# Weights laid out on the host in 8 KB rows, the first modulation taken k-tile by k-tile, and the context rows asked for one weight piece later

## What is computed

```
mod_lat = (silu_c @ ada_w[i] + ada_b[i])          # 6 x 2048 numbers: shift, scale, gate, twice
mod_ctx = silu_cc @ ada_w[i] + ada_b[i]
h_lat = modulate(rms_norm(x, norm_mix_g[i]), sh1, sc1)      # h * (1 + scale) + shift
h_ctx = modulate(rms_norm(ctx, norm_mix_g[i]), csh1, csc1)
if mixer == 0:
    q_l, k_l, v_l = project_qkv(h_lat, attn_w_qkv[j], attn_q_norm_g[j], attn_k_norm_g[j])
    k_c, v_c = project_kv(h_ctx, attn_w_qkv[j][:, D_MODEL:], attn_k_norm_g[j])
    o_lat = latent_attention(q_l, k_l, v_l, k_c, v_c) @ attn_w_o[j]
else:
    o_lat = fourier_mix(h_lat, fourier_w_o[j])
x = x + g1 * o_lat
x = x + g2 * sq_relu_mlp(modulate(rms_norm(x, norm_mlp_g[i]), sh2, sc2), mlp_w1[i], mlp_w2[i])
```

## Time and profile before

| | us |
|---|---|
| median of three runs | 2005.79 |
| the profiled execution | 2005.52 |
| its span (first to last instruction) | 2003.6 |
| PE busy in the span | 1965.9 (98%) |
| DVE busy | 1391.5 (69%) |
| ACT busy | 969.3 (48%) |
| DMA, mean over the span | 271 GB/s |

### The profile page before, as it was taken

The page is one execution under the profiler, slowest core; times in us unless marked ns, Lnnn a source line. Parts: engine busy times, 40 slices in busy tenths (PEclk is TensorE's granted clock), DMA queues, the critical chain, the costliest instruction groups (busy, mean ns, idle before and its releaser), DMA issues.

```text
span 2003.6 us, 24992 instructions
## 1 busy us (share of the span) xinstructions
PE 1965.9 (98%) x10188; PEld 1609.5 (80%) x10188; DVE 1391.5 (69%) x1424; ACT 969.3 (48%) x1265; POOL 110.9 (6%) x196
## 2 busy tenths in 40 slices
PE   6999989999999999999999999999999999999998
PEld 4677756778888888888888888788888888888886
DVE  3666998889867787788888675766666455555556
ACT  6432565455544455544444464555554454444444
POOL 1111001000000000000000000000000000000000
PEclk9999999999999999999999999999999999999999
DMA  9998768779989899799999626577776566555653
GB/s 359 338 378 319 277 257 297 272 252 323 353 293 348 313 360 364 262 367 363 355 395 383 219 85 193 175 252 253 257 251 220 187 192 210 189 192 198 218 190 126
DMA packets 152261, 542.80 MB, mean 271 GB/s; under 512 B 9393, under 2 KB 10577, under 8 KB 114641
## 3 DMA queue, kind: packets, MB, share of 16 engines
q1 hardware_dynamic: 119312, 335.77, 47.9%
q0 software_dynamic: 31744, 201.34, 27.1%
q10 hardware_dynamic: 1090, 4.09, 0.5%
HBM read 535.91 MB, written 2.10 MB: 269 GB/s over the span
## 4 chain that ended last, share of the span: by engine, by line
PE 94%; DVE 3%; ACT 1%; DMA 1%; issue 1%; POOL 0%; ACTq 0%; DVEq 0%; POOLq 0%
PE ps L2098 13%; PE ps L2036 12%; PE ps L2032 12%; PE ps L2035 11%; PE ps L2096 11%; PE ps L2099 6%; PE ps L1848 6%; PE ps L2095 6%; PE ps L1849 5%; PE ps L1850 5%; PE ps L2257 1%; PE ps L1913 1%; PE ps L2204 1%; DMA spare<-in_ada_w 1%; PE ps L2242 1%
## 5 line engine op out<-in xcount | busy, mean ns | idle before, releaser
L1201 DVE TENSOR_TENSOR w_lo<-raw,w_hi 128x1024 fp32r<-128x1024 f32 x616 | 749.5, 1223 | 467.9 <-ACT w_hi L727 467.6
L727 ACT ACTIVATE w_hi<-raw 128x1024 fp32r<-128x1024 f32 x616 | 649.4, 1059 | 845.7 <-PE ps L2036 345.8
L2098 PE MATMUL ps<-hh,w_hi 128*128 128x512 f32 x1088 | 427.5, 398 | 1.1 <-DVE hh L1627 1.1
L2032 PE MATMUL ps<-w_hi,hh 128*128 128x512 f32 x992 | 385.9, 389 | 0.0
L2036 PE MATMUL ps<-w_hi,hh 128*128 128x512 f32 x992 | 385.9, 389 | 0.0
L2035 PE MATMUL ps<-w_lo,hh 128*128 128x512 f32 x992 | 385.9, 389 | 0.0
L2096 PE MATMUL ps<-hh,w_hi 128*128 128x512 f32 x960 | 379.9, 396 | 0.0
L2099 PE MATMUL ps<-hh,w_lo 128*128 128x256 f32 x1088 | 302.9, 278 | 0.0
L2095 PE MATMUL ps<-hh,w_lo 128*128 128x256 f32 x960 | 267.5, 279 | 0.0
L2099 PEld LDWEIGHTS ps<-hh,w_lo 128*128 128x128 f32 x1088 | 205.7, 189 | 40.9
L2035 PEld LDWEIGHTS ps<-w_lo,hh 128*128 128x128 f32 x992 | 186.2, 188 | 38.9
(11 more groups left out here) (252 smaller groups left out, 1620.4 us busy)
## 6 DMA issues: line engine op xcount, KB each, us to landing
raw<-in_mlp_w SPq DMA_DIRECT2D x256, 1024.0 KB, 5.3
ada_raw<-in_ada_w POOLq DMA_DIRECT2D x151, 1024.0 KB, 6.2
spare<-in_ada_w POOLq DMA_DIRECT2D x29, 1024.0 KB, 6.6
raw<-in_attn_w_qkv SPq DMA_DIRECT2D x24, 1024.0 KB, 10.1
raw<-in_attn_w_o SPq DMA_DIRECT2D x16, 1024.0 KB, 5.7
raw<-in_fourier_w_o SPq DMA_DIRECT2D x16, 1024.0 KB, 5.1
g_row<-in_ada_w POOLq DMA_DIRECT2D x12, 1024.0 KB, 9.0
g_row<-gate_rows SPq DMA_DIRECT2D x48, 64.0 KB, 5.2
```

Source lines behind the costliest of these rows:

```text
L727: act.activation(w_slot(s)[0], raw[:, piece % RAW, s % 2, :], ACT.Copy).then_inc(hi_ready, 1)
L1201: nc.vector.tensor_tensor(lo, raw[:, s // 2 % RAW, s % 2, :], hi.bitcast(F32), ALU.subtract).then_inc(lo_ready, 1)
L2032: ins = mm(bank_of(tt, nb), h_hi[:, k % KT, tok], hi[:, cols], start=start, stop=False)
L2098: mm(both, w_hi[:, s % SPLIT, w], hh[:, k, :, :], start=(k == 0), stop=False, skip_group_check=True)
```

## The change

There are three parts.

**Layout.** The host now stores every w_qkv, w_o, Fourier and first MLP weight piece, and the 32 start pieces of ada_w, as 128 contiguous rows of 8 KB. The same bytes go to the same places in the buffers.

**Beginning by k-tile.** Start pieces 0 and 1 now hold shift and scale of k-tile 0, pieces 2 and 3 those of k-tile 1. Each k-tile has its own short chain: rows out (`first_rows`), columns (`first_cols` in two parts), shift and scale (`take_first_k`), modulated x (`shape_first`), low part (`lower_first`). `product(r, part)` runs the half of products 0 to 3 that needs k-tile 0 first, the other halves later. The second k-tile's rows and columns use PSUM bank 5, so turn_input(5) moves behind product 0.

**Order on SP.** Weight piece 0 now waits for start piece 0, weight piece 1 for start piece 2, and the context rows are issued behind piece 2 instead of piece 1.

```diff
+        def load_packed(piece, src):
+
+            load_piece(piece, src.rearrange("p (h n) -> p h n", h=2))
...
         sp.dma_start(ident[:, :], ident_in).then_inc(c_in, 16)
-        sp.wait_ge(ada_in[start_slot(1)], 16)
         for p in range(24):
-            if p < 6:
-                load_first(p)
-            else:
-                load_columns(p, wqkv_v[p // 6, column_block(p)])
-            if p == 1:
+            if p < 2:
+                sp.wait_ge(ada_in[start_slot(2 * p)], 16)
+            load_packed(p, w_qkv[p])
+            if p == 2:
                 sp.dma_start(c_rows[:, :, :], ctx_in[0].rearrange("(a p) d -> p a d", p=P)).then_inc(ctx_rows_in, 16)
...
-            pool.dma_start(dst, src).then_inc(ada_in[start_slot(n)], 16)
+            pool.dma_start(ring(start_slot(n)), ada_start[n]).then_inc(ada_in[start_slot(n)], 16)
...
+        def shape_first(kt):
+
+            act.wait_ge((a_first, a_ready)[kt], 1)
+            act.wait_ge(x_T_out, 1)
+            act.activation(xT[:, kt, :], xT[:, kt, :], ACT.Identity, bias=mod_col[:, kt:kt + 1],
+                           scale=a_col[:, 0, kt:kt + 1]).then_inc(mod_done, 1)
+            shaped[0] += 1
+            act.wait_ge(mod_done, shaped[0])
+            act.activation(h_hi[:, kt, :], xT[:, kt, :], ACT.Copy).then_inc((first_hi, hhi_ready)[kt], 1)
...
-        take_first(0, 0)
+        take_first_k(0)
         split_lo(0)
-        lower(0, 0)
+        lower_first(0)
+        take_first_k(1)
         split_lo(1)
+        lower_first(1)
         take_first(0, 1)
...
+        first_cols(0, (0, 1))
         first_piece(2)
         turn_input(0)
         turn_input(1)
         first_piece(3)
         turn_input(2)
-        first_cols(0)
-        for i in range(3, 6):
-            turn_input(i)
+        turn_input(3)
+        first_cols(0, (2, 3))
...
+        for r in range(4):
+            product(r, 0)
+        turn_input(4)
         for r in range(77):
-            product(r)
+            product(r, 1 if r < 4 else None)
+            if r == 0:
+                pe.wait_ge(start_mods, 2)
+                turn_input(5)
             if r == 1:
                 turn_input(6)
                 turn_input(7)
```

More of the change, by code:

```diff
@@ L851, in _ @@
         x_out(3)
+        shape_first(1)
         x_out(4)
@@ L1316, in take_first @@
             dve.wait_ge(vec_ready, 3)
[L1317 to L1319 removed]
+            for t, kt in enumerate(range(kts.start, kts.stop)):
+                at = slice(kt, 17 + kt, 16)
+                nc.vector.tensor_tensor(dst[:, at], ps[:, 6 - (kt == 1), 4 * t + n:4 * t + 4:2], bias_col[:, at],
+                                        ALU.add).then_inc((first_mods, start_mods)[t], 1)
+            dve.wait_ge(first_mods, 2 * c + n + 1)
             dve.wait_ge(start_mods, 2 * c + n + 1)
@@ L1853, in tile_out, with product @@
             return ps[:, bank0 + j // 2, (j % 2) * T:(j % 2 + 1) * T]
-        def product(r):
+        def product(r, part=None):
             p, cb, tt = product_at(r)
             c = r // 16
-            if r < 5:
+            if part == 1:
+                pass
+            elif r < 5:
                 pe.wait_ge(x_T_out, (1, 2, 3, 4, 7)[r])
@@ L1865, in product @@
             hi, lo = (h_hi, h_lo) if tt < 2 else (hc_hi, hc_lo)
-            pe.wait_ge(h_ready, 2 * c + 1 + tt // 2)
+            if part == 0:
+                pe.wait_ge(first_h, 1)
+            else:
+                pe.wait_ge(h_ready, 2 * c + 1 + tt // 2)
             tok = slice((tt % 2) * P, (tt % 2 + 1) * P)
@@ L1869, in product @@
             n = kts.stop - kts.start
-            for k in range(n):
+            for k in range(n) if part is None else (part,):
                 sl, b = (2 * p + k // 2, k % 2) if n == 4 else (2 * p + k, cb % 2)
@@ L1886, in first_piece, with first_cols @@
                 j = 32 * (k % 4)
-                ins = mm(ps[j:j + 32, 6, m * T:(m + 1) * T], silu[:, 8 * q + k, :], w[:, k, :], start=(q == 0 and k < 4),
+                ins = mm(ps[j:j + 32, 6 - (n // 2 == 1), t * T:(t + 1) * T], silu[:, 8 * q + k, :], w[:, k, :], start=(q == 0 and k < 4),
                          stop=(q == 1 and k >= 4), skip_group_check=True)
             ins.then_inc(ada_mm, 1)
-        def first_cols(c):
-            pe.wait_ge(rows_copied, c + 1)
-            pe.wait_ge(pick_ready, 2)
-            for f in range(4):
-                ins = mm(ps[:, 6, 2 * f:2 * f + 2], ada_rows[:, f * P:(f + 1) * P], pick_first[:, :], start=True, stop=True)
-            ins.then_inc(col_mm, 1)
+        def first_cols(c, part=(0, 1, 2, 3)):
+            if part == (0, 1):
+                pe.wait_ge(early_rows, 1)
+                pe.wait_ge(pick_ready, 2)
+            else:
+                pe.wait_ge(rows_copied, c + 1)
+            for f in part:
+                ins = mm(ps[:, 6 - (c == 0 and f > 1), 2 * f:2 * f + 2], ada_rows[:, f * P:(f + 1) * P], pick_first[:, :], start=True,
+                         stop=True)
+            ins.then_inc(col_first if part == (0, 1) else col_mm, 1)
         def ada_piece(n):
@@ L2427, with by_columns, qkv_pieces, start_pieces @@
         "attn_k_norm_g", "attn_w_o", "fourier_w_o", "mlp_w1", "mlp_w2", "final_norm_g"]
+def by_columns(w):
+    return w.reshape(4, 4, P, -1, 512).transpose(3, 0, 2, 1, 4).reshape(-1, 4, P, D)
+def qkv_pieces(w):
+    first = w.reshape(8, 2, P, 3, NC).transpose(0, 3, 2, 1, 4)[0:2].reshape(6, P, D)
+    columns = by_columns(w)
+    return np.concatenate([first, np.stack([columns[column_block(p), p // 6] for p in range(6, 24)])])
+def start_pieces(w):
+    rows = w[:, 0:2 * D]
+    first = rows.reshape(2, 8, P, 2, 8, 2, P).transpose(4, 5, 0, 2, 1, 3, 6)[0:2].reshape(8, P, D)
+    later = rows.reshape(4, 4, P, 2, 4, 512).transpose(4, 3, 0, 2, 1, 5)[1:4].reshape(24, P, D)
+    return np.ascontiguousarray(np.concatenate([first, later]))
 def kernel(**inputs):
@@ L2444 @@
             a = a[:, TOKENS]
+        if name == "attn_w_qkv":
+            a = qkv_pieces(a[0])
+        if name in ("attn_w_o", "fourier_w_o"):
+            a = by_columns(a[0])
+        if name == "mlp_w1":
+            a = _np.stack([by_columns(a[0]), by_columns(a[1])])
         a = _np.ascontiguousarray(a)
```

69 lines of the change are left out of this document (37 added, 32 removed).

## The result

| kernel | median, us | lowest to highest | runs |
|---|---|---|---|
| before | 2005.77 | 2003.09 to 2007.70 | 16 |
| changed | 2009.35 | 2006.91 to 2012.54 | 16 |

The ratio is 1.0020, with a 95% interval of 1.0013 to 1.0026: the change costs 2.6 to 5.2 us. The profiled execution of the changed kernel is the fastest of its 16, 2006.91 us with a span of 2005.1 us, 1.5 us above the one of before. How 1.5 us there and 3.6 us between the medians belong together is told further down.

The account below looks back on a forecast made before the run. PE bounds the kernel beyond 60 us, so only the beginning can pay. From 2005.5 us, 0.5 + 0.9 - 2.2 + 1.4 + 0.9 = +1.5 gives 2007.0 us, range 2001.5 to 2010.5.

Parts of the forecast that it names:

- The vectors, forecast at 22.0: Beginning: small vectors, queued behind x on ACT's queue, land 7.4 us after x, at 22.0 us; PE waits for them.
- Context rows: Beginning: context rows land near 32.1 us behind weight pieces 1 and 2, with 8 us of cover; taken as 0.
- So x lands 1.0 / 0.418 = 2.4 us later, and 0.8 us more: Beginning: equal turns with 8 KB start pieces, plus weight piece 0, delay x's landing to 14.6 us.
- x starved: Rival, chance 0.18: piece 0 precedes x, which gets one turn of three, landing at 18.5 us (border 16.5); 2010.3 us.
- PE from 22.1 us: PE's work from the small vectors to product 0: 7.7 us after overlap, product 0 at 29.8, 0.5 us later.
- +0.9 for the turns: After product 0 begins: two turns of x, formerly done by then, still remain, costing 0.9 us.
- -2.2: Around 30.7 us: early halves remove the 0.50 us wait and the half-clock stretch worth 1.7 us; 2.2 us won.
- +1.4: Before product 4's second k-tile: fewer matmuls cover the fourth slot, so the w_lo wait grows to 1.9 us, losing 1.4.
- half of a slow stretch: After the longer w_lo wait: an even chance of a second half-clock stretch of 1.7 us, counted as 0.9 us.
- From 60 us on PE waits for no DMA, and shorter POOL issues and faster rows are hidden by PE: 0: Rest of the kernel beyond 60 us: no change, 0 within 0.5 us either way.
- Early inputs: Rival, chance 0.27: x keeps its lead, vectors land about 18.9 us, product 0 begins 3.1 us earlier; 2003.0 us.
- Nothing from the layout: Rival, chance 0.05: pieces arrive as before, only the k-tile order acts, product 0 near 27 us; 2004.2 us.

Follow-up runs that it names:

- e5: The changed kernel with the context rows issued behind weight piece 1 again instead of piece 2; 2009.97 us, ratio 1.0019.
- e9: The kernel before with the 8 KB layout and x issued by GpSimd ahead of the start pieces, old order otherwise; 2004.17 us, ratio 0.9995.
- e10: The kernel before with only x issued by GpSimd ahead of the start pieces, without the 8 KB layout; 2005.39 us, ratio 1.0004.
- e3: The changed kernel with x issued by GpSimd ahead of the start pieces instead of on ACT's queue; 2003.08 us, ratio 0.9988.
- e1: The changed kernel with the 32 start pieces back in short runs of 1 and 2 KB; 2009.42 us, ratio 1.0021.
- e2: The changed kernel with the four small-vector DMAs on SP's queue behind the identity matrix; 2010.66 us, ratio 1.0024.
- e7: The changed kernel with x issued by GpSimd first and, from the twentieth on, start pieces ahead of VectorE's loads; 2002.61 us, ratio 0.9986.
- e11: The changed kernel with start pieces in short runs and, from the twentieth on, ahead of GpSimd's loads for VectorE; 2008.21 us, ratio 1.0014.
- e12: The kernel before with 8 KB layout, x first on GpSimd, start pieces from the twentieth ahead of VectorE's loads, no early halves; 2001.27 us, ratio 0.9985.
- e4: The kernel before with the 8 KB layout of weights and start pieces alone, old order everywhere; 2009.75 us, ratio 1.0023.

## Why the prediction came out as it did

The measured 3.6 us (2.6 to 5.2) are more than my 1.5. The direction and the mechanism of the beginning were right and the sizes too small. At product 0 the changed kernel is 1.7 us behind, where I had 0.5; to the context product another 1.5 us, where I had 1.0; to the k turn another 0.4 us, where I had 0 within 0.5. Of the 1.2 us that are missing at product 0, the vectors are 0.2, x's lateness 0.45, and the lengths on PE the rest, as told below.

**Right.** Turns packet by packet: in the kernel before, from 6 to 10 us, queue 10 moved 138 packets and queue 0 144; after, from 9 to 12 us, 79 and 79. The vectors, forecast at 22.0, were turned at 22.33, behind a new wait on PE with everything queued behind it. That their time came out so well is partly luck: x ahead of them landed 1.6 us later than forecast, and they followed it after 6.1 us instead of 7.4. The 0.50 us wait behind product 0 and the lower clock at 30.7 us went. The wait for w_lo before the second k-tile of product 4 was forecast at 1.9 us and was 1.87. Context rows: POOL's next start piece, which waits for them, was issued at 32.8, and they were first read at 42.22; e5 confirms the 0. Start pieces in 8 KB rows do move faster where they stand alone, 424 against 351 GB/s in e9 and e10. The 418 that I used for them was read from queue 1 alone, where 12 of the 213 packets were below 8 KB, and not from a mixture with 4 KB rows; the size was right.

**The term that was mis-sized: "So x lands 1.0 / 0.418 = 2.4 us later, and 0.8 us more".** x landed 4.8 us later (16.19 against 11.36), not 3.2. I put x's whole lead in the kernel before down to the packet sizes. In truth 0.85 MB of it went by before queue 0 moved a byte. I had named the earlier start of a contiguous piece under "x starved", but gave it only there. The weight piece also came into the turns at 8.3 us of issue instead of the 9.2 that I estimated. x at 16.2 lies between the forecast (14.6) and the rival's border (16.5).

**The step that follows, "PE from 22.1 us", 7.7 us to product 0, was 8.6.** 0.45 us of it is PE's wait for ACT, on which the rows that the columns need stand behind x's squares: the same lateness of x once more. Without it the stretch is 8.2 us, the plain sum of my lengths: the 0.5 us that I took off for overlap at the seams was not there. Product 0 came at 30.95 instead of 29.8.

**From product 0 to the context product I had +1.0 us, made up of +0.9 for the turns, -2.2, +1.4 and half of a slow stretch.** Measured: 31.41 us against 29.93, +1.5, in an execution that did have the stretch, for which my terms give +1.8. In e5, without the stretch, it was 29.78, -0.15, for which they give +0.1. So these terms were sized right. The 1.7 us of the slow stretch that I booked as won were not won in the profiled execution: the stretch was moved, from 31 to 43 us, not removed. The windows after:
```profile
40.00:45.00 5.00, 3.70 (x11) 2.96 (x12) 3.74 (x4) 4.80 (x11) 0.00 (x0) 0.77 1.01 423
45.00:50.00 5.00, 5.00 (x33) 3.59 (x31) 3.49 (x8) 4.75 (x14) 0.00 (x0) 0.89 0.89 370
```

**The step that had no margin: "From 60 us on PE waits for no DMA, and shorter POOL issues and faster rows are hidden by PE: 0".** In the changed kernel it held within the 0.5 us that I gave it: one wait of 0.3 us appeared (ada_raw, between 90 and 245 us). But a start piece is issued when a slot comes free and lands 9.6 us later in the median of the changed kernel (g_row, nine pieces), and 13 us in e3 beside other loads, when it is needed. In e1 there are waits of 0.5, 1.5 and 1.5 us, in e2 2.6, in e3 1.5 and in e9 1.6 us. e7 and e11, which put these pieces ahead of the loads beside them, show none, and e12 none from 90 us on. I had not looked at how near the kernel before was to such a wait.

**How 1.5 and 3.6 us agree.** At the context product the changed kernel is 3.1 us behind, at the k turn 3.5. It ends 1.5 us behind in the profiled execution because the kernel before lost time in its own, in two stretches of lower granted clock that the changed one had not. The first is at the MLP of the first layer. The same stretch of work, before and then after:
```profile
445.00:452.00 7.00, 5.58 (x26) 4.73 (x26) 6.55 (x15) 5.92 (x10) 0.00 (x0) 0.76 0.24 61
```
```profile
448.70:455.70 7.00, 5.58 (x34) 4.75 (x34) 6.55 (x15) 6.87 (x11) 0.00 (x0) 1.00 0.26 69
```
From the first turn of the MLP's input, at 443.16 and 446.88 us, to the first late matmul at 1139.76 and 1142.11 us, it is 696.6 us before and 695.2 us after: 1.4 us. The second is at the MLP of the second layer:
```profile
1282.00:1289.00 7.00, 5.33 (x24) 4.56 (x25) 5.80 (x14) 6.47 (x13) 0.00 (x0) 0.76 0.09 20
```
```profile
1284.40:1291.40 7.00, 4.75 (x29) 4.08 (x30) 6.06 (x15) 6.73 (x14) 0.00 (x0) 1.00 0.13 25
```
There the turns of x at 1283.43 and 1285.79 us are 2.36 us apart, and those at 1291.86 and 1293.43 us 1.57: 0.8 us. The changed kernel has a stretch of its own from 274.8 to 278.2 us (granted 0.50, where the other had 1.00); it is 3.5 us behind ahead of it and 3.7 us at 446.88, so this one cost at most 0.2 us. Without the three the profiled pair would differ by 1.5 + 1.4 + 0.8 - 0.2 = 3.5 us, next to the 3.6 between the medians. The stretch at 447 us is in two of the fourteen profiled executions, those of before and of e3; how often a kernel has it, one execution of each does not tell. That the profiled execution differs by the 1.5 us that I had forecast is thus the sum of errors of opposite sign, not a confirmation.

**The rivals.** Early inputs did not happen, but e3 made them happen by an edit, and its 2003.08 us is what that rival said of the time (2003.0), with product 0 at 25.5, 1.2 us ahead of what the rival gives, and then less of the lead left. x starved was right in its first step: the contiguous start piece 0 began at once and was multiplied at 8.45 us, 4.2 us earlier. But x kept every second turn until 12 us and every third after it, and landed at 16.2, not 18.5. In time that rival's 4.8 us are nearer to the measured 3.6 than my 1.5. Nothing from the layout is out: in e4 it alone costs 1.0023, and with x first it gives 2.1 us at product 0 (e9 against e10). What I had overlooked is that the layout's loss has a cheap cure.

**What is left open.** The layout with x late (e4) and the order by k-tile with short runs (e1) each cost as much as both together. For e4 the cause is shown, by e9 and e3: x's place. For e1 it is not: e11 takes away the late start pieces and stays 1.0 to 4.6 us above the kernel before. The weight pieces in 8 KB rows, which e1 has too, are in e9 and e12 as well and cost nothing there; SP's new order, with weight piece 1 behind start piece 2, was not tried by itself.

## To carry to other kernels

A faster transfer in a beginning where several queues compete is first of all a reordering: list what each queue lands and when, and put first (in one queue, by issue order) what the longest chain needs, here x, before judging the layout. When a chain ahead gets shorter, look at every ring behind it for its margin, since a wait of zero in the trace says nothing of how close the next one is. Compare single profiles by milestones, stretch by stretch, and set aside all stretches of lower clock that only one of them has, before a difference of 1 to 2 us is given a cause.

## What the runs showed of the hardware that I had not expected

- **GpSimd's first DMA starts late when its runs are short.** GpSimd's first start piece, in runs of 1 KB, issued at 1.3 us, moved nothing before 5.5 us; in rows of 8 KB it moved 0.65 MB between 2.5 and 5.5 us. e1 and e11, with short runs again, repeat it: queue 0 moved nothing up to 5.5 us. Its issue takes 1.04 us of GpSimd in short runs and 0.66 in long ones, which is not the difference.
- **The same waits, with and without a lower clock.** e9 and e12 have the same beginning and the same waits of 1.65 and 0.50 us at product 0. From 28.5 to 32 us, in e9 and then in e12:
```profile
28.50:32.00 3.50, 3.26 (x9) 2.55 (x10) 1.64 (x4) 1.82 (x3) 0.63 (x2) 0.65 1.02 419
```
```profile
28.50:32.00 3.50, 3.50 (x20) 2.98 (x21) 1.32 (x2) 2.26 (x5) 0.43 (x1) 1.00 1.00 417
```
  In e9 a stretch at 1.2 instead of 2.4 GHz follows, in e12 not. From product 0 to the start piece behind product 8, that is 16.5 against 14.9 us: this stretch costs 1.6 us. The changed kernel and e5 give the same, 31.41 against 29.78 us. Others cost less: 1.4 and 0.8 us at the two MLPs of the kernel before, at most 0.2 us at 274.8 us in the changed one. So an idle time of this length comes before such a stretch in some executions and not in others, and a single profile can be 1.6 us off for it.
- **Sixteen matmuls of a start piece take 1.93 or 1.07 us, both under a granted clock of 1.00.** In the changed kernel the first three took 1.93, the fourth 1.36 us and all later ones 1.07; in e3 the third already took 1.07, with PE busy from 15.3 to 18.4 us ahead of it. The column of the granted clock does not show this, only the lengths do, and it makes up 0.6 of the 0.8 us by which product 0 differs between e5 and the changed kernel, which are the same on PE up to there. What makes the difference is not shown.
